# An attention pipeline on one core: the transposes of unit t-2 issued ahead of the scores of unit t

## The reference

```python
s_loc = einsum('bnqkgd,bnjkd->bnkgqj', qb, kb) * scale
s_ctx = einsum('bnqkgd,bckd->bnkgqc', qb, k_ctx) * scale
s_loc = where(allowed, s_loc, -inf)
m = maximum(maximum(s_loc.max(-1), s_ctx.max(-1)), sink_l)
p_loc, p_ctx = exp(s_loc - m), exp(s_ctx - m)
denom = p_loc.sum(-1) + p_ctx.sum(-1) + exp(sink_l - m)
o = (einsum('bnkgqj,bnjkd->bnkgqd', p_loc, vb) + einsum('bnkgqc,bckd->bnkgqd', p_ctx, v_ctx)) / denom
```

## Time and profile before

| what | value |
|---|---|
| median of 3 runs | 5123.26 us (5112.72 to 5138.3) |
| the profiled execution | 5130.85 us, span 5129.1 us |
| TensorE busy over the span | 85% |
| VectorE, ScalarE, GpSimd busy | 31%, 22%, 15% |
| mean granted TensorE clock | 0.907 |

### The profile page before, as it was taken

One profiled execution on the slowest core, in us unless ns is written; L12 is line 12 of the kernel. 1 busy time (PEld: TensorE's weight loads), 2 busy tenths in 40 slices (PEclk: granted clock), 3 DMA queues, 4 the chain that ended last, 5 costly groups with the idle time before them and its releaser, 6 DMA issues. The chain is left out here.

```text
span 5129.1 us, 74458 instructions
## 1 busy us (share of the span) xinstructions
PE 4337.1 (85%) x28872; PEld 2808.1 (55%) x28872; DVE 1568.6 (31%) x2365; ACT 1108.3 (22%) x1499; POOL 751.6 (15%) x555
## 2 busy tenths in 40 slices
PE   6999867887998899757779996888778999999962
PEld 3666655665665688646656664453434444444431
DVE  2000265443232100645542412452221111111127
ACT  1000233322122111333321213340201111111110
POOL 1111101001222322000102220000050000000014
PEclk8999977878999899878879998999779999999985
DMA  4334312231221222210002221000107999999966
GB/s 177 144 143 159 133 32 92 96 150 51 78 90 53 87 94 82 73 49 23 27 23 82 81 78 35 9 30 31 68 3 292 360 359 362 357 359 357 358 252 249
DMA packets 170080, 715.25 MB, mean 139 GB/s; under 512 B 26882, under 2 KB 28675, under 8 KB 134019
## 3 DMA queue, kind: packets, MB, share of 16 engines
q1 hardware_dynamic: 119714, 536.83, 29.3%
q10 hardware_dynamic: 25632, 93.33, 4.5%
q0 software_dynamic: 24512, 81.84, 4.4%
HBM read 584.95 MB, written 126.98 MB: 139 GB/s over the span
## 5 line engine op out<-in xcount | busy, mean ns | idle before, releaser
L400 PE MATMUL ps<-s_proj_hS,s_proj_wS 128*128 128x512 f32 x3216 | 762.3, 398 | 62.2 <-POOL s_proj_wS L312 62.2
L400 PEld LDWEIGHTS ps<-s_proj_hS,s_proj_wS 128*128 128x128 f32 x3216 | 605.6, 189 | 223.6 <-ACT s_proj_wS L361 63.1
L1806 PE MATMUL ps<-s_mix_hS,s_mix_wS 128*128 128x512 f32 x1536 | 394.9, 413 | 40.1 <-POOL s_mix_wS L1665 35.5
L1806 PEld LDWEIGHTS ps<-s_mix_hS,s_mix_wS 128*128 128x128 f32 x1536 | 291.4, 190 | 134.9 <-issue 67.5
L2720 PE MATMUL ps<-s_exp_gu,keep_hT 128*128 128x512 f32 x736 | 340.1, 605 | 14.8 <-DMA s_exp_gu<-in_w_gu_dram 12.9
L2704 PE MATMUL ps<-s_exp_wd,s_exp_aT 128*128 128x512 f32 x736 | 332.9, 595 | 1.9 <-ACT s_exp_aT L2630 1.9
L2725 PE MATMUL ps<-s_exp_gu,keep_hT 128*128 128x512 f32 x736 | 330.9, 592 | 0.0
L1665 POOL TENSOR_TENSOR s_mix_wS<-s_mix_w,s_mix_wS 128x1024 fp32r<-128x1024 f32 x96 | 230.7, 2404 | 582.3 <-ACT s_mix_wS L1674 582.3
L312 POOL TENSOR_TENSOR s_proj_wS<-s_proj_w,s_proj_wS 128x1024 fp32r<-128x1024 f32 x67 | 162.8, 2433 | 690.1 <-ACT s_proj_wS L361 690.0
L340 DVE COPY s_proj_o<-ps 128x512 f32<-128x512 f32 x66 | 45.6, 692 | 707.4 <-PE ps L400 707.4
L2670 DVE TENSOR_TENSOR s_exp_sg<-s_exp_sg,ps 128x256 f32<-128x256 f32 x92 | 38.7, 421 | 660.1 <-ACT s_exp_sg L2651 660.1
(11 more groups left out here) (432 smaller groups left out, 6081.8 us busy)
## 6 DMA issues: line engine op xcount, KB each, us to landing
s_exp_gu<-in_w_gu_dram SPq DMA_DIRECT2D x184, 1024.0 KB
s_exp_wd<-in_w_down_dram SPq DMA_DIRECT2D x92, 1024.0 KB, 9.0
yrow<-keep_hT ACTq DMA_DIRECT2D x92, 512.0 KB
s_proj_wa<-in_w_ada_dram SPq DMA_DIRECT2D x72, 512.0 KB, 4.3
s_proj_w<-in_w_in_dram SPq DMA_DIRECT2D x66, 512.0 KB
proj<-s_proj_o ACTq DMA_DIRECT2D x66, 512.0 KB, 2.6
yrow<-keep_xT SPq DMA_DIRECT2D x4, 8192.0 KB
s_mix_w<-in_w_in_dram SPq DMA_DIRECT2D x64, 512.0 KB
```

The lines of the kernel that those rows point to most:

```text
L400: mm = pe.matmul(k.ps[:, 6 + half if last else 2 * b + half, :], wS[:, b, x, t, :], hS[:, y, t, half * HALF:(half + 1) * HALF], start=(t = ...
L1806: mm = pe.matmul(k.ps[:, bank, :], wS[:, b, u, x, :], src[:, v, x, :], start=(x == 0 and u + v == 0), stop=(x == KT - 1 and u == 1))
```

## The change

TensorE's loop calls the same two functions in the other order. All instructions, waits and buffers stay as they are, and so do the loops of the other engines.

```diff
             for t in range(NU + LAG_V):
+                if 0 <= t - LAG_T < NU:
+                    turned(t - LAG_T)
                 if t < NU:
                     scores(t)
-                if 0 <= t - LAG_T < NU:
-                    turned(t - LAG_T)
                 if t - LAG_V >= 0 and (t - LAG_V) % 2:
                     values((t - LAG_V) // 2)
```

## The result

| | before | changed |
|---|---|---|
| median of 4 runs each | 5126.38 us (5112.72 to 5138.3) | 5191.94 us (5186.61 to 5205.39) |
| ratio of times | | 1.0142, 95% interval 1.0121 to 1.0162 |
| the profiled execution | 5130.85 us, span 5129.1 | 5205.39 us, span 5203.6 |
| loop, VectorE's start of slot 1 to that of slot 31 | 145.8 us | 224.3 us |

The account below looks back on a forecast made before the run. VectorE and TensorE taking turns, neither near 100% busy, were taken to bound the attention loop. Closed chain +47 us and falling clock +25 us made +72 us, forecast as 5195 us on the median, range 5160 to 5225.

Parts of the forecast that it names:

- point 1: TensorE's attention loop: scores of unit t queue behind the waits of t-2's transposes, making every slot one closed chain.
- point 2: Full attention slots: 6.69 us with and without values, the values' product hidden; a full pair costs 3.03 us more.
- S: From the first of TensorE's scores to VectorE's start of that slot: 1.40 us wide, 1.18 us narrow.
- points 3 and 4: Narrow slots 5.37 us; 18 wide steps at 6.69 and 12 mixed at 6.03 make the loop 192.8 us, +47.0 us.
- point 5: TensorE's clock falls in the 4.17 us idle stretch of nearly every pair: 1.7 us x 15 pairs, +25 us.
- The clock rival: In the attention loop the chain closes but the clock stays up: only +47 us, 5170 us; chance 0.23.
- The rival of a mostly low clock: In the attention loop the clock is low most of the time: above +92 us, some 5230 us; chance 0.09.
- the rival of no effect: The attention stage doesn't feel TensorE's new order: 5123 us; chance 0.05.
- The faster rival: Transposes first let copies and values' product start sooner, removing TensorE's 30.4 us idle before transposes: 5093 us; chance 0.03.
- D: From VectorE's first instruction of a slot until its last lets TensorE go on: 4.05 us wide, 3.17 us narrow.
- T: TensorE's transposes in one slot: 1.24 us wide, 1.02 us narrow.

Follow-up runs that it names:

- after_again: The changed kernel run once more on another chip, beside the kernel before: ratio 1.0157, loop 224.4 us.
- wait_only: Kernel before, scores still first, with the transposes' waits put ahead of the scores: ratio 1.0072, loop 184.8 us.
- wait_fill3: Kernel before with the transposes' waits ahead of the scores, plus 3 extra matmuls in each slot without values: ratio 1.0023, loop 168.5 us.
- fill7: Changed kernel plus 7 extra matmuls, results unused, in each slot without values: ratio 1.0091, loop 194.9 us.
- fill3: Changed kernel plus 3 extra matmuls, results unused, in each slot without values: ratio 1.0095, loop 197.3 us.
- swap_n: Kernel before with transposes put ahead of scores only in the slots without values: ratio 1.0083, loop 178.8 us.
- swap_v: Kernel before with transposes put ahead of scores only in the slots with values: ratio 1.0074, loop 180.4 us.
- lead: Changed kernel with scores made one unit ahead, transposes still first in each slot: ratio 0.9949 to the kernel before, loop 123.5 us.
- lead_old: Kernel before, scores still first in each slot, with scores made one unit ahead: ratio 1.0019, loop 148.7 us.

## Why the prediction was right

The time (5191.9 against 5195), the direction and the mechanism held. That the time came within 3 us is partly luck. The forecast adds 72 us, the loop grew by 78.6, and the medians moved by only 65.6 us on this chip and by 77.6 on that of after_again, with equal loops.

- **The wait behind which the scores are queued** (point 1). Shown by wait_only with wait_fill3: the wait alone, with nothing moved, costs about 23 us, with the clock at 1.00 from 3300 us on.
- **The full slot of 6.69 us, with and without values** (point 2). Measured 6.69 in all wide slots at full clock, in the changed kernel, in fill7 and in fill3. (The pair of the earlier trace rows ends in a slot of a narrow unit and takes 10.13 us itself; fully wide pairs before take 10.34 to 10.35, as the sum with S = 1.40 has it.) That the values' product is hidden holds as well. The idle stretch was worked out as 4.17 us and is 4.13 by the matmuls' row.
- **The sum of +47.0 us, with the middle for the 12 mixed slots** (points 3 and 4). The loop at full clock was to be 192.8 us; fill7 has 194.9, with about 1.6 us of filler in it. Step by step from fill3, with its two slow first steps taken from the same place in its second round (5.59 and 5.94 us), it is 193.3. The 12 mixed steps are 6.07 us on average, against the middle of 6.03.
- **The clock, +25 us** (point 5). Right in kind; it cost 224.3 - 193.3 = 31 us, a quarter more. The term was 15 alike pairs at 1.7 us. Behind the 13 gaps from slot 5 on, a slot lost 1.85 us on average, 24 us in all: among the fully wide ones the low stretch lay over all of the work in some (8.94 us, +2.25) and over three quarters in others (8.32, +1.63). Two slots with values, beside narrow units, lost another 1.3 us together. And in the first three steps from slot 1 the clock was low throughout, up to the last of the third step's scores: 7.63, 7.98 and 8.01 us instead of 5.59, 5.94 and 6.30, which is 5.8 us. The kernel before has a low clock there too, but only up to some 3284 us; the changed one has it up to 3300 us, by windows of 2 us. That the clock would fall in nearly every gap held, but the reason given for it, that the new gap is longer than one behind which it fell, is weaker than it looked: swap_n, swap_v and wait_only show equal gaps with and without a fall.
- **The clock rival** (the clock stays up, 5170) is the kernel fill7 and not this one. The rival of a mostly low clock needed more than +92 us and fails by the loop's +78.6, and the rival of no effect with it. The faster rival (product and copies sooner) failed at the point named: the transposes wait for VectorE even longer when they stand first, 83.9 us by the weight loads' row instead of 30.4. Its idea isn't empty, though: with the scores made one unit ahead, transposes first is the better order, by 25 us over scores first (lead and lead_old).

By the Trainium skill ("TensorE: Matmul & The Clock Gate", section "HAM oscillation — how this bites in real kernels") every pass of such a loop pays, for which I had an estimate of up to 33 us; the loop's 31 us agree with it. In swap_n, swap_v and wait_only, whose gaps are shorter than the 4.13 us here, not every pass pays.

## What to carry to other kernels

In a loop in which two engines hand units to each other, look at each wait for what is queued behind it: an instruction without that need, put behind it, closes a chain. The price is worked out from what was overlapped before and is no longer (here a further D + T + S, less the values' product that is now hidden: 3.03 us a pair), not from the 1.24 us of work moved. Make what feeds the waiting engine one unit earlier before you reorder within a slot: the same order cost 79 us with the scores of the newest unit and saved 22 with those of the next. And when a new idle stretch of TensorE appears, price the clock over the work behind it; some useless matmuls in the gap tell quickly how much of a loss is the clock's.

## What the runs showed of the hardware

- TensorE's clock came back from 0.50 to 1.00 in the midst of the unbroken work behind the gap and fell again in the next gap of 4.13 us, so that slots of 6.69 and 8.3 to 8.9 us alternate; and the pattern repeated to 0.1 us on another chip (loops 224.3 and 224.4).
- Equal idle pieces had unequal effects. In swap_n two pieces of 1.06 and 1.72 us brought the clock down in one pair and not in the next; in wait_only single pieces of 2.95 us did so in some pairs only, and in swap_v pieces of 2.88 us.
- Six extra matmul instructions (1.56 us by their row) in each second slot kept it at 1.00 from 3300 to 3440 us, in a loop in which TensorE still idled for 0.70 and 1.87 us around them.
- Transposes run at either clock: 10 take 1.24 us at 1.00 and 2.32 us at 0.50, x1.87. The Trainium skill ("TensorE: Matmul & The Clock Gate", section "Part 4: PE-mode transpose") says that the full clock doesn't engage in transpose mode; in these rows it holds through the transposes. The kernel doesn't show what transposes alone would do.
